# First-pass score fills of the 64-row attention heads: 64-row products and products over all 128 rows

## What is computed

```python
def block_attention(q, k, v, scale):
    ...
    def one_block(qblk):
        s = jnp.einsum('bqgrd,bkgd->bgrqk', qblk, k).astype(jnp.float32) * scale
        p = jax.nn.softmax(s, axis=-1).astype(v.dtype)
        return jnp.einsum('bgrqk,bkgd->bqgrd', p, v)
...
# MLA (4 heads): q, k have MLA_NOPE + MLA_ROPE = 64 + 32 = 96 numbers
o_a = block_attention(q_a, k_a, v_a, MLA_QK ** -0.5).reshape(b, L, MLA_W) * jax.nn.silu(a_g)
...
# GQA (4 heads, 2 key heads): q, k have GQA_HD = 64 numbers
o_d = block_attention(q_att, k_att, v_att, GQA_HD ** -0.5).reshape(b, L, GQA_W) * jax.nn.silu(d_g)
```

## Time and profile before

| | us |
|---|---|
| median of 3 runs | 4141.85 (4140.83 to 4143.78) |
| profiled execution | 4141.9 |
| its span, first to last instruction | 4140.2 |
| TensorE busy | 3649.6 (88%) |
| VectorE busy | 2899.0 (70%) |
| ScalarE busy | 1502.1 (36%) |
| the fills' products of 512 columns, in `p1` (992 of them) | 305.4, mean 475 ns |

### The profile page before, as it was taken

The page is one execution under the profiler, slowest core; times in us unless marked ns, Lnnn a source line. Parts: engine busy times, 40 slices in busy tenths (PEclk is TensorE's granted clock), DMA queues, the critical chain, the costliest instruction groups (busy, mean ns, idle before and its releaser), DMA issues. The chain is left out here.

```text
span 4140.2 us, 51260 instructions
## 1 busy us (share of the span) xinstructions
PE 3649.6 (88%) x18304; PEld 2584.7 (62%) x18304; DVE 2899.0 (70%) x5006; ACT 1502.1 (36%) x3066; POOL 178.9 (4%) x263
## 2 busy tenths in 40 slices
PE   6798969957999999986969989796879999999599
PEld 1797858735566555445759977685645665545377
DVE  1454968967677788856755479686867777888576
ACT  0661114465333344441136411243923333444311
POOL 0000000000000000000100000000010000000010
PEclk8899989968899999997989999897979999999799
DMA  7553536633111222215435354576141121220343
GB/s 282 176 180 120 180 117 188 176 114 86 24 41 42 43 42 45 43 43 175 162 128 193 114 174 151 149 194 180 30 94 35 43 42 37 49 49 6 114 162 132
DMA packets 340871, 450.83 MB, mean 109 GB/s; under 512 B 134153, under 2 KB 272777, under 8 KB 323745
## 3 DMA queue, kind: packets, MB, share of 16 engines
q1 hardware_dynamic: 323424, 324.62, 25.0%
q0 software_dynamic: 17216, 123.22, 11.4%
HBM read 291.64 MB, written 156.10 MB: 108 GB/s over the span
## 5 line engine op out<-in xcount | busy, mean ns | idle before, releaser
L2007 ACT ACTIVATE attn_Pb<-attn_ST 128x1024 f32<-128x1024 f32 x544 | 547.2, 1026 | 888.7 <-PE attn_ST L1894 528.6
L2031 DVE TENSOR_REDUCE attn_mx<-attn_p 128x1 f32<-128x1024 f32 x496 | 607.4, 1225 | 284.4 <-PE attn_p L1835 277.5
L2075 DVE TENSOR_TENSOR attn_acc<-attn_acc,attn_Pb 128x1024 f32<-128x1024 f32 x480 | 584.0, 1217 | 31.1 <-ACT attn_Pb L2007 29.7
L1906 PE MATMUL attn_OT<-attn_Pb,attn_V 128*64 128x512 f32 x2176 | 545.3, 616 | 0.0
L518 PE MATMUL chan_b<-chan_hh,w_in_hi 128*128 128x256 f32 (+1 forms) x1152 | 329.2, 286 | 0.5 <-DVE w_in_lo L377 0.5
L519 PE MATMUL chan_b<-chan_hh,w_in_lo 128*128 128x256 f32 (+1 forms) x1152 | 326.5, 283 | 0.0
L520 PE MATMUL chan_b<-chan_hl,w_in_hi 128*128 128x256 f32 (+1 forms) x1152 | 326.4, 283 | 0.0
L1835 PE MATMUL attn_p<-attn_K,attn_Q 64*128 64x512 f32 (+1 forms) x992 | 305.4, 475 | 14.6 <-DVE attn_mx L2031 13.9
L837 DVE SCALAR_TENSOR_TENSOR gate_GY<-gate_win,gate_fw,gate_GY 128x1096 f32<-128x1096 f32 x240 | 310.5, 1351 | 0.4
L1835 PEld LDWEIGHTS attn_p<-attn_K,attn_Q 64*128 64x128 f32 (+1 forms) x992 | 131.0, 191 | 269.9 <-DVE attn_mx L2031 214.5
L1906 PEld LDWEIGHTS attn_OT<-attn_Pb,attn_V 128*64 128x64 f32 x2176 | 129.8, 137 | 227.9 <-issue 194.5
(11 more groups left out here) (331 smaller groups left out, 6813.6 us busy)
## 6 DMA issues: line engine op xcount, KB each, us to landing
gate_ht<-scratch_HT POOLq DMA_DIRECT2D x34, 1024.0 KB, 6.2
head_ht<-scratch_HT POOLq DMA_DIRECT2D x34, 1024.0 KB, 5.4
mod_w<-in_w_mod SPq DMA_DIRECT2D x16, 1536.0 KB, 12.3
scratch_HT<-chan_hh SPq DMA_DIRECT2D x34, 512.0 KB, 2.7
scratch_HT<-chan_hl SPq DMA_DIRECT2D x34, 512.0 KB, 3.8
scratch_G<-gate_GT SPq DMA_DIRECT2D x34, 512.0 KB, 3.6
out_G<-scratch_G SPq DMA_DIRECT2D x34, 512.0 KB, 4.8
scratch_QM<-head_QST SPq DMA_DIRECT2D x34, 384.0 KB, 3.5
```

The source lines that it names most:

```text
L1906: mm = pe.matmul(OT[o * HD:(o + 1) * HD, :], V[par][:, kt, :], Pb[unit % NPB][:, o * 512:(o + 1) * 512], start=(kt == 0), stop=(kt == NKT ...
L2007: act.activation(Pb[unit % NPB][:, :], ST[unit % 2][:, :], ACT.Exp).then_inc(q["exp_done"], 1)
L2031: ins = dve.tensor_reduce(mx[:, t, w:w + 1], made[:, :], AX.X, ALU.max)
L2075: ins = dve.tensor_tensor(sums[:, :], sums[:, :], prob[:, :], ALU.add)
```

## The change

For a 64-row head, both products of a fill are over all 128 rows: `Q1` (queries' high part over their low part) with `K1` (keys' high part twice). That is keys' high part times both parts of the queries, where it was high times high alone. `Q2` is no longer read by a fill. The 96-row heads' fills stay as they are. No other line changes, and the instructions of all engines stand in the same order with the same waits; only the operands' rows differ. Line numbers behind the edit are lower by 8.

```diff
--- before.py
+++ after.py
@@ -1814,24 +1814,16 @@
                     for i in range(NT_Q):
                         t = i // 2 + i % 2 * (NT_Q // 2)
                         q0 = b * QB + t * P
-                        if is_mla(h):
-                            qt, kt = Q1[par][0:QK, q0:q0 + P], K1[par][0:QK, LAT:KEYS]
-                        elif t < NT_Q // 2:
-                            qt, kt = Q1[par][0:HD, q0:q0 + P], K1[par][0:HD, LAT:KEYS]
-                        else:
-                            qt, kt = Q2[par][HD:P, q0:q0 + P], K1[par][HD:P, LAT:KEYS]
+                        rows_ = slice(0, QK if is_mla(h) else P)
+                        qt, kt = Q1[par][rows_, q0:q0 + P], K1[par][rows_, LAT:KEYS]
                         mm = pe.matmul(out[:, t * P:(t + 1) * P], qt, kt, start=True, stop=True)
                 else:
                     t, w = divmod(r - 1, WIDE)
                     q0 = b * QB + t * P
                     for c in range(2):
                         k0 = w * 1024 + c * 512
-                        if is_mla(h):
-                            qt, kt = Q1[par][0:QK, q0:q0 + P], K1[par][0:QK, k0:k0 + 512]
-                        elif c == 0:
-                            qt, kt = Q1[par][0:HD, q0:q0 + P], K1[par][0:HD, k0:k0 + 512]
-                        else:
-                            qt, kt = Q2[par][HD:P, q0:q0 + P], K1[par][HD:P, k0:k0 + 512]
+                        rows_ = slice(0, QK if is_mla(h) else P)
+                        qt, kt = Q1[par][rows_, q0:q0 + P], K1[par][rows_, k0:k0 + 512]
                         mm = pe.matmul(out[:, c * 512:(c + 1) * 512], qt, kt, start=True, stop=True)
                 mm.then_inc(q["p1_done"], 1)
```

## The result

The changed kernel takes 4157.83 us, the median of 6 runs (4151.41 to 4164.53), beside 4142.26 of the kernel before (4135.61 to 4146.16, 6 runs). The ratio is 1.0036, with a 95% interval of 1.0026 to 1.0046. The forecast was 4157.9 and slower by 0.39%. The measured difference is 15.6 us, and its interval runs from about 10.8 to 19.1 us, so the agreement of the two times within 0.1 us is luck: the kernel before came out 0.4 us higher than the forecast had taken it, and the difference 0.4 us lower.

What follows compares the result with a forecast made beforehand. TensorE's order of products was taken to set a pass's length; 1.00 us a pass, beside a sum of 1.02, over 16 passes gave +16.0 us on 4141.9, so 4157.9 us (0.39% slower), range 4151 to 4167.

Steps and rivals of the forecast that it cites:

- The second way: Whole passes with 96-row scores: 53.81 us with 96-row fills less 52.81 with 64-row fills (pass 7), 1.00 us a pass.
- The sum by place: Costs of a pass's eight even fills, eight odd fills and fill 0 added from trace rows: 1.02 us a pass.
- The even fills: Eight fills a pass that follow the values: +0.05 us each.
- The odd fills: Eight fills a pass that stand before the values and mostly follow scores: +0.04 us each.
- Fill 0: A pass's first fill, eight products of 128 columns in sequence instead of four overlapped pairs: +0.30 us a pass.
- The stand-in: 96-row fill prices used for 128-row fills, since 128-row scores after values take the same 0.34 us.
- margins of 0.4 us: VectorE's maxima of even and odd fills would be ready 0.4 us before the next fill needs them.
- The clock: First rival: TensorE's clock falls in every second of the 16 affected passes, 1.6 us each, 4170.8 us; chance 7%.
- The hidden cost: Second rival: VectorE decides and TensorE has slack, so the longer fills do not show, 4142 us; chance 6%.
- The third rival: Overlap worth a whole product, no edge cheaper: 16 fills a pass lose 0.23 us each, 4206 us; chance 2%.
- The disagreement that the prediction saw: By the skill's rule a 64-row pair would take about 0.23 us, where the trace shows 0.43.
- The fourth rival: 128-row fills pay no extra at the values' edges, -0.68 us a pass, 4131 us; chance 3%.

Runs made afterwards that it cites:

- e9: The changed kernel without the second product of the 64-row heads' fills 1 to 16; a single execution took 4105.96 us, a 64-row pass 42.21 us.
- e2: The kernel before with only the even fills of the 64-row heads over 128 rows; a single execution took 4142.80 us, a 64-row pass +0.26 us.
- e5: The kernel before without the second product of the 64-row heads' fills 1 to 16; a single execution took 4145.45 us, a 64-row pass 44.56 us.
- e4: The kernel before with both products of the 64-row heads' fills 1 to 16 on rows 0 to 63, so without overlap; ratio 1.0184.
- e6: The kernel before with the denominators in two halves and VectorE's reciprocal moved back; 4125.59 us, ratio 0.996.
- e7: The changed kernel with the denominators in two halves and VectorE's reciprocal moved back; 4143.63 us, ratio 0.9998.
- e8: e4 with the denominators in two halves and VectorE's reciprocal moved back; ratio 1.0103 to the kernel before.

## Why the prediction was right, and where its terms were off

**The bound.** TensorE's order sets the pass: right. The waits after are the same one of 0.3 us, and e9 shows a pass that shortens by 3.45 us when TensorE gets 16 products less.

**The second way.** Pass 7 as a trial of the change in reverse gave 1.00 us a pass; measured are 0.95 in 64-row passes and 0.87 in pass 7 itself. This step carried the forecast, and it was 5% too high for a 64-row pass and 15% for pass 7. Pass 7 after the change takes 53.68, so 0.13 of its distance to the 53.81 of a 96-row pass did not belong to the height of the fills. The two kinds of pass differ in more than the fills, which the prediction overlooked: at their end `max_row` turns eight tiles of 97 columns for a 96-row head (`mtm`) and of one column for a 64-row head (`mtg`). In the kernel before, pass 2 of the first layer and then pass 7 of the second show it:

```profile
1210.30 1.11 PE L1864 MATMUL attn_p<-ident,attn_mtm 128*97 128x128 f32 x8
1211.34 1.08 PE L1906 MATMUL attn_OT<-attn_Pb,attn_V 128*64 128x512 f32 x4
```

```profile
3503.07 1.03 PE L1864 MATMUL attn_p<-ident,attn_mtg 128*1 128x128 f32 x8
3504.03 1.08 PE L1906 MATMUL attn_OT<-attn_Pb,attn_V 128*64 128x512 f32 x4
```

To the next group it is 1.04 us and 0.96, so 0.08 of the 0.13 is this turn, which the change does not touch.

**The sum by place.** It gave 1.02, and 0.95 came. The even fills were mis-sized: 0.05 each in the rows, 0.03 in e2. The row was one place, at 96-row scores, and its difference was multiplied by 8; in e2 the eight places add between 0.00 and 0.07 us. The odd fills' 0.04 is 0.03 for seven of them and 0.15 for fill 3, whose place behind the denominators had no row of its own in the sum. Fill 0 was right (0.30, measured 0.32). The errors of the even and the odd fills have opposite signs, so the total hides them in part.

**The stand-in.** 128 rows pay at the edges what 96 pay: right, with 0.34 and 0.24 in the two products of an even fill (0.74 for the two, less 0.40).

**VectorE.** It stays clear. e9 tries about half of the prediction's margins of 0.4 us: there each fill comes some 0.22 us sooner after the one before it, and no wait is added.

**The rivals.** The clock did not fall in 64-row passes; that it can was shown in e4 and e5. The hidden cost did not come. The third rival took the overlap to be worth 0.23 and no edge to get cheaper: its first half is right (e5, e9: 0.01 against 0.22), its second is wrong. The Trainium skill, "TensorE: Matmul & The Clock Gate", section "Measured speedup vs the span model", is borne out: it gives a group of such products one product's duration and some 4 ns for each further one. Here the pair's record lasts 0.50 us with two products as with one, and the second adds 0.01 us to what it holds TensorE for. The disagreement that the prediction saw was its own: it put the 0.23 us between the starts of full products in a row in the place of that duration, and the 0.43 is what e5's lone product holds TensorE for, too. The fourth rival fell with the 0.34 behind the values.

**Outside attention** lengths were to stay. In the profiled execution they did not quite: passes 0 to 13 of the two layers together are up by 15.6 us (1411.9 to 1427.4) and the span by only 10.8, so the rest of the program was shorter by 4.8 us, although it holds pass 14 of each layer, whose fills the change makes longer as well. It is one execution of each kernel, and the medians are 15.6 apart; why the other stages vary stays open.

## What to carry to other kernels

Two half-height products side by side save nearly a whole product, but a single pair between full-height products pays for its edges, and keeps about 0.04 us of 0.21. Four short pairs in a row (fill 0) keep more, 0.32 us, or 0.08 a pair at a quarter of the length: grouping pairs where the buffers allow is worth a trial, which was not made here. When a kernel has both variants in one trace, compare whole passes before adding up differences of 0.01 us, and look for what else differs in them: here the turn of the maxima was 0.08 of the 1.00 us. And look at what TensorE does just before its clock falls: here a run of one-column products, cut in two, gave 0.4%, as much as the change under study cost.

## What was not expected of the hardware

The granted clock fell in 64-row passes that had less to do or the same products one after another, where the kernel before shows no fall. e5's 64-row passes have TensorE's starts within 0.15 us a pass of the kernel before's, and only the second product of each pair missing, and one pass in each layer fell, with 46.12 us for 44.56. In the profiles of the kernel before and of the changed one, 24 such passes (8 to 13 of each layer) never did. But e9's 12 passes without the second products did not fall either, and in the kernel before, passes 2 and 3 of the first layer have the same products, the one without a fall (53.81 us) and the other with one (55.43). So the products alone do not settle it; where a pass stands in time may count as well, and no run here separates the two. With the run of one-column products cut in two, no pass from 1 to 13 fell in e6, e7 or e8. Pass 0 is another case: it has no denominators, starts at the lower clock and waits for VectorE's maxima (1.3 us before its second fill in the kernel before), and its clock is low for a part of it in all kernels.
